# Order of TensorE's work in the attention slots of a hybrid decoder layer: scores, map transpositions and filling products

## The reference

```
proj = rmsnorm(x) @ w_in                    -> q, k, v (4 heads), cb, cc, cu
q, k = rotary(rmsnorm(q)), rotary(rmsnorm(k))    per head two branches of 64 values
a    = softmax(q0 k0^T / 8) - lam * softmax(q1 k1^T / 8)     causal, one map per head
attn = rmsnorm(a @ v) * (1 - lambda_init)
conv = rmsnorm(cb * (3-tap causal convolution of cc * cu))
h    = x + concat(attn, conv) @ w_out
out  = h + top-2-of-32-experts(rmsnorm(h)), group chosen first
```

## Time and profile before

| | |
|---|---|
| median of three executions | 1179.57 us |
| the profiled execution: its own time / its span | 1181.24 / 1179.5 us |
| TensorE busy over the span | 1106.0 us (94%) |
| VectorE / ScalarE / GpSimd busy | 842.5 / 657.5 / 352.0 us |
| attention stage, 310 to 554 us: TensorE / VectorE / ScalarE busy | 218.45 / 171.28 / 128.27 us |
| mean granted TensorE clock over the execution | 0.98 of full speed |

### The profile page before, as it was taken

How to read it: one execution, slowest core, us unless ns; L and a number is a source line. 1 busy time by engine, 2 the same in 40 slices (tenths; PEclk the granted TensorE clock), 3 DMA queues, 4 the chain that set the end, 5 groups by cost and what they waited for, 6 DMA issues and landing times.

```text
span 1179.5 us, 15247 instructions
## 1 busy us (share of the span) xinstructions
PE 1106.0 (94%) x5629; PEld 866.4 (73%) x5629; DVE 842.5 (71%) x1110; ACT 657.5 (56%) x901; POOL 352.0 (30%) x431
## 2 busy tenths in 40 slices
PE   4999999999969999889789999999999999999995
PEld 3998989889758877768667777777777777766673
DVE  6644353343686776767669899889889889888894
ACT  5412121121465655543448778778778877777773
POOL 2332333323431111121103433443343343222220
PEclk9999999999999999999689999999999999999998
DMA  8012030302310222322789999999999999999972
GB/s 246 14 40 68 19 89 1 89 19 83 114 24 24 85 90 90 126 90 107 281 283 343 382 372 373 380 372 364 386 375 367 369 366 359 373 372 362 373 307 39
DMA packets 76506, 254.16 MB, mean 215 GB/s; under 512 B 17808, under 2 KB 42384, under 8 KB 51856
## 3 DMA queue, kind: packets, MB, share of 16 engines
q1 hardware_dynamic: 69264, 236.37, 54.0%
q0 software_dynamic: 7168, 16.79, 6.0%
HBM read 240.55 MB, written 20.97 MB: 222 GB/s over the span
## 4 chain that ended last, share of the span: by engine, by line
PE 43%; DMA 7%; DVE 3%; ACT 1%; issue 1%; POOL 0%; POOLq 0%; ACTq 0%; DVEq 0%
PE banks L2093 9%; PE banks L2095 9%; PE banks L2094 9%; DMA raw<-in_w_gate 6%; PE banks L2110 4%; PE banks L2112 4%; PE banks L2114 4%; PE banks L2069 2%; DVE wlo L2014 1%; PE banks L2078 1%; DMA rows<-xn_rows,table_i 1%; ACT whi L1963 1%; DMA xn_rows<-hn 0%; PE banks L1636 0%; DMA out<-y_sb,table_i 0%
## 5 line engine op out<-in xcount | busy, mean ns | idle before, releaser
L2014 DVE TENSOR_TENSOR wlo<-raw,whi 128x2048 fp32r<-128x2048 f32 x190 | 428.0, 2287 | 52.0 <-ACT whi L1963 51.7
L1963 ACT CAST whi<-raw 128x2048 fp32r<-128x2048 f32 x188 | 354.3, 1911 | 39.2 <-DMA raw<-in_w_gate 23.5
L2093 PE MATMUL banks<-whi,rT_hi 128*96 128x512 f32 x512 | 207.4, 405 | 6.1 <-DVE wlo L2014 5.2
L1945 POOL DMA_INDIRECT out<-y_sb,table_i x32 | 149.0, 4656 | 200.7 <-ACT y_sb L1981 195.5
L2095 PE MATMUL banks<-whi,rT_lo 128*96 128x512 f32 x512 | 203.4, 397 | 0.0
L2094 PE MATMUL banks<-wlo,rT_hi 128*96 128x512 f32 x512 | 202.3, 395 | 0.0
L2093 PEld LDWEIGHTS banks<-whi,rT_hi 128*96 128x96 f32 x512 | 83.3, 163 | 41.9 <-DVE wlo L2014 6.3
L2095 PEld LDWEIGHTS banks<-whi,rT_lo 128*96 128x96 f32 x512 | 83.1, 162 | 36.5
L2094 PEld LDWEIGHTS banks<-wlo,rT_hi 128*96 128x96 f32 x512 | 83.7, 164 | 31.4
L1936 POOL DMA_INDIRECT rows<-xn_rows,table_i x30 | 49.6, 1652 | 190.8 <-PE banks L2069 183.3
L862 ACT ACTIVATE qk_sq<-banks 128x256 f32<-128x256 f32 x32 | 12.3, 384 | 154.0 <-PE banks L1494 154.0
(11 more groups left out here) (248 smaller groups left out, 2049.5 us busy)
## 6 DMA issues: line engine op xcount, KB each, us to landing
raw<-in_w_gate SPq DMA_DIRECT2D x64, 1024.0 KB, 23.5
raw<-in_w_up SPq DMA_DIRECT2D x64, 1024.0 KB, 24.0
raw<-in_w_down SPq DMA_DIRECT2D x64, 1024.0 KB, 25.1
c_raw<-in_w_in SPq DMA_DIRECT2D x12, 512.0 KB, 3.8
q_raw<-in_w_in SPq DMA_DIRECT2D x12, 512.0 KB, 6.1
x_stage<-in_x SPq DMA_DIRECT2D x8, 512.0 KB, 7.9
wo_raw<-in_w_out SPq DMA_DIRECT2D x2, 2048.0 KB, 7.7
h_sb<-in_x SPq DMA_DIRECT2D x8, 512.0 KB, 4.4
```

What stands on the lines that cost most here:

```text
L1945: pool.indirect_dma_start(out=s.out_rows, out_offset=bass.IndirectOffsetOnAxis(ap=s.table_i[:, e:e + 1], axis=0), in_=s.y_sb[e % 2][:], in ...
L1963: act.copy(s.w_hi[i % HI][:], s.raw[i % RING][:]).then_inc(s.hi_ready, 1)
L2014: dve.tensor_tensor(s.w_lo[i % RING][:], s.raw[i % RING][:], s.w_hi[i % HI][:].bitcast(F32), ALU.subtract).then_inc(s.lo_ready, 1)
L2093: pe.matmul(o, s.rT_hi[e % 2][:, c, :], hi[:, c4, :], start=(c == 0), stop=False)
```

## The change

Three edits to TensorE's list in the attention slots; no other engine's list changes, and no instruction is added or taken away:

1. `score(g, 1)` comes straight behind `score(g, 0)` (and `turn_h`, where there is one), ahead of `turn_maps(g - 1, 0)`.
2. The filling product is cut in two halves of six products. The first half (k = 0, 1) stands between `turn_maps(.., 0)` and `turn_maps(.., 1)`, the second (k = 2, 3) behind it.
3. The waits at the head of `multiply_out` go with the first half.

```
-            def multiply_out(i, q):
+            def multiply_out(i, q, ks=(0, 1, 2, 3)):
                 n, cols = q % 2, half_cols(q % 2)
                 o = ps[:, 6 + n, :]
-                if q == 0:
...
+                if 0 in ks:
+                    if q == 0:
+                        pe.wait_ge(mc_ready, i + 1)
...
+                    if q == 1 and i >= 1:
+                        pe.wait_ge(h_ready, 2 * i)
+                        if i < NT - 1:
+                            pe.wait_ge(hnT_copied, 2 * i)
...
-                for k in range(4):
+                for k in ks:
                     if q == 2:
                         pe.wait_ge(oT_ready, HEADS * i + k + 1)
...
-                ins.then_inc(half_done, 1)
+                if 3 in ks:
+                    ins.then_inc(half_done, 1)
...
             for g in range(SLOTS_2):
+                i, q = fill_at(g)
                 score(g, 0)
                 if turn_b_at(g) is not None:
                     turn_h(turn_b_at(g), 1)
+                score(g, 1)
                 if g >= 1:
                     turn_maps(g - 1, 0)
-                score(g, 1)
+                if i is not None:
+                    multiply_out(i, q, (0, 1))
                 if g >= 1 and tile_head(g - 1)[0] >= 4:
                     turn_maps(g - 1, 1)
                 if g == SLOTS_2 - 2:
                     count_first()
-                i, q = fill_at(g)
                 if i is not None:
-                    multiply_out(i, q)
+                    multiply_out(i, q, (2, 3))
```

More of the change, by code:

```diff
@@ L1608, in weigh @@
                 ins.then_inc(pv_done, 1)
-            def multiply_out(i, q):
+            def multiply_out(i, q, ks=(0, 1, 2, 3)):
                 n, cols = q % 2, half_cols(q % 2)
                 o = ps[:, 6 + n, :]
-                if q == 0:
[L1614 to L1629, removed]
-                for k in range(4):
+                if 0 in ks:
+                    if q == 0:
+                        pe.wait_ge(mc_ready, i + 1)
+                        if i == 0:
+                            pe.wait_ge(wo_lo_ready, 4)
+                            pe.wait_ge(k_ready, PROJ - 1)
+                        else:
+                            pe.wait_ge(h_ready, 2 * i - 1)
+                    if q == 1 and i == 0:
+                        pe.wait_ge(k_ready, PROJ)
+                    if q == 1 and i >= 1:
+                        pe.wait_ge(h_ready, 2 * i)
+                        if i < NT - 1:
+                            pe.wait_ge(hnT_copied, 2 * i)
+                        else:
+                            pe.wait_ge(oT_ready, BEFORE_LAST + 1)
+                    if q == 2 and i == 0:
+                        pe.wait_ge(wo_lo_ready, 8)
+                for k in ks:
                     if q == 2:
```

## The result

| | before | after |
|---|---|---|
| median of 7 executions each, in turn on one chip | 1180.77 us | 1193.22 us |
| lowest to highest | 1176.73 to 1184.12 | 1191.01 to 1197.78 |
| profiled execution: its own time / its span | 1181.24 / 1179.5 us | 1197.78 / 1195.9 us |

The ratio is 1.0108 with a 95% interval of 1.0089 to 1.0126: slower by 12.5 us. The forecast was 9.3 us slower (1189, range 1177 to 1196). The profiled execution of the kernel after is the slowest of its seven, 4.6 us above their median, so its span overstates the difference.

A forecast was written before the change was run, and what follows sets the result against it. The bound was taken to be the ScalarE and VectorE chain from the first map transpositions to the routing products, not TensorE's work. Terms 4.1 + 3.9 + 3.3 - 2.0 gave 9.3 us longer: 1189 us, range 1177 to 1196.

The forecast's parts named there:

- (a): Slots 9, 13, 17, 21, 25, 29: first map transpositions come one score group later, paid in full: 4.1 us longer.
- (b): Slots 9, 13, 17: halved filling product delays ScalarE's second copy of maps 1.3 us each: 3.9 us longer.
- (c): Slots 10, 14, 18: ScalarE's copy of the second maps starts 1.1 us later each: 3.3 us longer.
- (d): Slots 11, 12, 15, 16, 19, 20: later transpositions fit into TensorE's existing waits, other waits replace them: counted 0.
- (e): Gains counted: waits filled in slots 1, 6 and 31, and ScalarE's slack at slot 21: 2.0 us shorter together.
- the 8 I named as a mark: Routing products' waits for ma_lo were to grow from 3.0 us in 6 to about 8 us or more.
- TensorE's clock: Attention stage: one to three more half-clock stretches possible, 0 to +5 us, left out of the likeliest time.
- rival 3: Attention stage: the sum holds and the clock falls in two or three more stretches: 1192 to 1195 us; chance 0.13.
- Rival 1: Attention stage: TensorE is the bound, the chain has slack; 5 to 7 us faster, 1172.7 to 1174.6; chance 0.12.
- Rival 2: Attention stage: only (a) on the path, second copy hidden; 3.7 us longer or nothing, 1180 to 1183.3; chance 0.20.

The follow-up runs named there:

- after, kept busy: Kernel after plus unused 512-column products in TensorE's stops ahead of routing products and `turn_h`; 1188.01 us, ratio 1.0066 to the kernel before.
- before, kept busy: Kernel before plus unused 512-column products in TensorE's stops, slots 2 and 3 included; 1180.06 us, ratio 0.9989 to the kernel before.
- first two experiments: Kernel before, changed only in slots 9, 13, 17, 21, 25, 29: second-branch scores earlier (1184.20 us, 1.0027); separately, filling product halved (1188.03 us, 1.0071).
- third experiment: Kernel before with scores first and halved filling product only in slots 10, 14, 18, 22, 26, 30; 1181.05 us, ratio 1.0012.
- fourth experiment: Kernel before with the new order in all slots except 9, 13, ..., 29 and 10, 14, ..., 30; 1180.88 us, ratio 1.0009.
- last version: Kernel before with maps ahead of `turn_h`, TensorE kept busy, scores first in slot 1, filling product halved in slot 6; 1171.58 us, ratio 0.9929.
- its repetition: The unchanged kernel after, measured and traced once more against the kernel before; 1190.08 us, ratio 1.0092.
- second experiment: Kernel before with only the filling product halved (`split`), in slots 9, 13, 17, 21, 25, 29; 1188.03 us, ratio 1.0071.
- kept-busy form: Kernel before with halved filling product in slots 9, 13, ..., 29, plus unused products in TensorE's stops; 1180.29 us, ratio 0.9999.

## Why the prediction was right, and where its size was off

This table lays the traces side by side. A section runs from the start of the routing products of one slot B to those of the next; the first one from the start of attention (all in us, differences of starts). The forecast column is my sum, distributed. The last row is the time at half clock, in us.

| section | before | after | after, kept busy | before, kept busy | kept busy: difference | forecast |
|---|---|---|---|---|---|---|
| to slot 9 | 72.56 | 74.96 | 76.28 | 72.06 | +4.2 | +1.0 |
| 9 to 13 | 34.36 | 38.92 | 37.37 | 34.39 | +3.0 | +3.3 |
| 13 to 17 | 32.41 | 38.31 | 35.17 | 32.42 | +2.8 | +3.2 |
| 17 to 21 | 31.28 | 33.98 | 30.78 | 30.11 | +0.7 | +1.3 |
| 21 to 25 | 28.12 | 26.88 | 26.95 | 26.53 | +0.4 | +0.5 |
| 25 to 29 | 27.10 | 26.88 | 26.16 | 25.87 | +0.3 | +0.3 |
| 29 to the end of the slots | 18.37 | 17.91 | 17.90 | 19.92 | -2.0 | -0.3 |
| all | 244.20 | 257.84 | 250.61 | 241.30 | +9.3 | +9.3 |
| at half clock | 13.6 | 27.2 | 10.2 | 6.8 | +3.4 | |

**What bounds the kernel** was right: the chain from the first map transpositions over ScalarE and VectorE to the routing products. Lengthening it (first two experiments) cost time with TensorE's work unchanged, closing waits off it gave nothing that the total shows, and shortening it gave 3.4 us, again with TensorE's work unchanged. Step by step:

- (a) right: ScalarE's idle time ahead of mapsT in slot 13 grew by 0.75 us and the copy is 0.82 later against the copy of h; +3.2 us (0.7 to 5.7) where 4.1 (3.7 with slot 21's slack) was said.
- (b) right in the trace: 2.62 and 2.61 us for a predicted 2.67. All six filling products of slots B wait for the copy of h, 6.9 us, at most 1.3, as said.
- (c) right within 0.25 us: 0.99, 0.91 and 0.85 us in the third experiment, 0.96 in slot 14 of the kernel after kept busy, for 1.1.
- (d) right in the main: 1.0009 for everything outside B and C. The mapsT waits went and the mc_lo waits came, with waits of `turn_h` that I had not named. From slot 9 to 13, where neither kernel is at half clock, the fourth experiment is 0.45 us longer than before where I had said 0.
- (e) half right: slots 1, 6 and 31 closed 1.7 us of waits, 1.04 us of it (slots 1 and 6) seen as time in the last version, none in the total of the fourth experiment; slot 21's slack was not taken.
- The routing waits grew to 6.2 us, not to the 8 I named as a mark: those of slots 9, 13 and 17 grew (0.45, 0.84 and 0.62 to 1.32, 1.84 and 1.73), slot 29's by 0.3, those of 21 and 25 stayed. I had TensorE standing still about 2 us longer in each wide slot B; ahead of the routing products it is 0.9 to 1.1 us.

**The term that was mis-sized is TensorE's clock**, which I left at nothing in the likeliest time and put into the upper end with 0 to +5 us. By the medians it is 3 to 5 us: 11 to 12.5 without, 7.8 with the clock held behind slot 9. The traces of after and its repetition have 27.2 us at half clock in the attention stage each, in the same six places within 2 us; before had 13.6 in four. The 13.6 more would cost half of it, 6.8 us, if all the time were spent on TensorE's path. It is in the second to fourth line of the table: the sections from 9 to 21 are 1.6, 3.1 and 3.2 us longer than with TensorE kept busy, for 3.4, 6.8 and 6.8 us at half clock. (From 21 to 25 the kernel before is at half clock for 3.4 us and after is not, hence the lower number of after in the fifth line.)

The cause is the one that I had named and not priced: step (b) adds about a microsecond to TensorE's stop ahead of the narrow routing products of slots 9, 13 and 17. What the clock did in or behind those products, over all thirteen traces:

| stop ahead of the routing products of slots 9, 13, 17 | places | half clock behind it |
|---|---|---|
| 1.3 to 1.85 us (after, its repetition, second experiment) | 9 | 8, five of them for 6.8 us |
| 0.4 to 1.0 us (before, the other experiments without added products) | 15 | 6, all for 3.4 us |
| 0.5 us and less, filled with added products (five kernels) | 15 | 0 |

So a longer stop makes the fall likelier and longer, and no single length decides it: in slot 9 of the second experiment TensorE stood for 1.32 us and the clock stayed full, in slot 17 of the kernel before it stood for 0.62 and the clock fell. This also explains the second experiment, whose waits there are 1.32, 1.85 and 1.72 us. The first one, at most 0.9 us, had one stretch of 3.4 us each in slots 13 and 17 and stayed near its sum.

**That 9.3 comes back in the table is in part luck.** The kernel after kept busy has 6.8 us more at half clock in the first section, the kernel before kept busy 3.4 us in the last. From slot 9 to 29, where neither has any, the difference is 7.1 us and my sum has 8.6. With the half-clock time priced at half its length the whole would be 7.6 instead of 9.3 (an estimate from the last row of the table, section by section: 9.3 - 3.4 + 1.7). So the chain was put about 1.5 to 1.7 us too high and the clock, in the traces, about 6 us too low (13.6 - 7.6, an estimate as well); these two misses have opposite signs. What happened is the sum and rival 3 together, at 1190 to 1193 us.

Rival 1 (TensorE the bound, 5 to 7 us faster) is refuted by the slots outside B and C and by the kernel with `split` in slots B, which got faster when work was added to TensorE. The Trainium skill (Perfetto Trace Analysis, "Optimization Strategy") says to find the gaps on the engine that one optimizes, to find out what each waits for, and to make that start sooner or finish faster. The runs here agree: the version that made ScalarE's input earlier won 3.4 us. The reordering closed the gaps by standing other work in front of what the chain waits for, and lost. Rival 2 (only the first edit on the path) falls with the second experiment and, at a held clock, with its kept-busy form: 1.27 and 1.24 us longer from slot 9 to 13 and from 13 to 17.

The Trainium skill (TensorE: Matmul & The Clock Gate, "A second HAM failure mode: psum-queue depth-cycling") has frequent micro-idles between groups of products as enough for a swinging clock. The fourth experiment does not test this rule: 3.3 us of small waits for the maps went, but others took their place (24.9 us of waits in all for 25.1), and the time at half clock grew from 13.6 to 20.4 us. Filling the stops ahead of the routing products, and of `turn_h` in slots 25 and 29, took it from 23.8 to 6.8 us and the ratio from 1.0071 to 0.9999, which goes the way of the rule. What small stops alone do to the clock stays open.

**The first and the last section.** The first is 4.2 us longer where I said 1.0. Between the two kept-busy kernels the half-clock time in it is 10.2 against 3.4 us, which costs up to 3.4, enough for the rest. (The kernel before kept busy has added products in slots 2 and 3, the other has none ahead of slot 9.) First the kernel after kept busy, then the kernel before kept busy:
```profile
309.91:386.19 76.28, 65.52 (x381) 52.95 (x380) 52.69 (x91) 42.31 (x98) 17.13 (x42) 0.93 0.19 58
```
```profile
309.73:381.79 72.06, 65.17 (x391) 52.65 (x390) 53.46 (x91) 42.00 (x98) 17.10 (x42) 0.98 0.21 61
```
The fourth experiment has the new order up to slot 8, the old one in slot 9, and the same 10.2 us: 74.09 us. So slot 9 costs 76.28 - 74.09 = 2.2 us of the 2.3 predicted. The last section's -2.0 goes with a half-clock stretch behind 533 us in the kernel before kept busy, which the other lacks. Open is why the clock falls behind some of the stops under 1 us and not behind others.

## What to carry to other kernels

In this kernel most waits of the busiest engine were worth nothing, because what they waited for was itself fed by that engine's own earlier output. Before filling such a wait, follow the releaser one step back: if it is another engine that was fed by this one, put its input first and let the filling work stand behind it, not in front. And price the new stop that a move creates twice: once as time, once as what the clock does in the work behind it.

## What the runs showed of the hardware

- Products of 512 columns that compute nothing of use made no kernel slower and two quicker (one of the two only if compared with the first measurement of the kernel after). Ahead of the routing products and of `turn_h` they raised the granted clock from 400 to 520 us from 0.94 to 1.00 in two kernels, and gave back 3 to 5 us (1.0108 or 1.0092 to 1.0066) and 8.5 us (1.0071 to 0.9999).
- The same instructions can run at either clock. Six kernels have the code of the kernel before up to slot 8; in three of their traces TensorE is at half clock around 347 to 350 us, in three it is not. The kernel with `split` in slots B is one of the first three: at 347 us its clock was at half; in the profiled execution of the kernel before it was full. First this kernel, then the kernel before:
```profile
347.00:348.00 1.00, 1.00 (x5) 0.94 (x6) 0.00 (x0) 1.00 (x3) 0.00 (x0) 0.50 0.00 0
```
```profile
345.60:349.00 3.40, 2.26 (x20) 2.19 (x20) 1.85 (x5) 3.30 (x7) 0.13 (x1) 1.00 0.01 2
```
  One profiled execution therefore does not settle a term of up to 1.7 us for one stretch. The six places of the kernel after did come back in its second trace, behind the longest stops among others.
- The same code behind the attention stage took 621.8 to 628.2 us in thirteen traces of it, and 627.3 and 621.8 us in two traces of one kernel.
